# Two normalisations opened by a rough mean, a gather on chip, and hidden chunks in buffers of their own

## The chip, the core and the metric

The kernel runs on one core of one Trainium2 chip. The metric is the device time of one execution in microseconds (us), the median of several. Engines are named as in the profile: PE is TensorE (its weight loads are PEld), DVE is VectorE, ACT is ScalarE, POOL is GpSimd, and SP issues most DMAs.

## The reference

One inference step of a two-layer decoder on 264 token rows (256 of a prompt, 8 samples) of 1024 features, all in float32. What matters here is the end of each sub-layer and the start of the mixture of experts:

```python
def _layernorm(x, g, b):
    mu = jnp.mean(xf, -1, keepdims=True)
    var = jnp.mean(jnp.square(xf - mu), -1, keepdims=True)
    return (xf - mu) * lax.rsqrt(var + EPS) * g + b
...
x = _layernorm(ALPHA * x + mix, ln1_g, ln1_b)        # after each mixer
ffn = (silu(x @ w1) * (x @ w3)) @ w2                  # layer 0: dense, 2816 hidden
ffn = sum over the 2 of 8 experts that the router picks of the same form   # layer 1, 3584 hidden
x = _layernorm(ALPHA * x + ffn, ln2_g, ln2_b)
```

So there are four normalisations, numbered 0 to 3: after the first mixer, after the dense feed-forward, after the second mixer, and at the end.

## The kernel before

Everything is held with features on the 128 partitions: x is `X`, eight chunks of 128 features by 264 tokens. A float32 product is done as three passes on rounded halves (`split_product`, L555 to L557): weights and inputs are each split into a high part (rounded by ACT) and the rest (subtracted by DVE). ACT writes the high parts of a weight tile from the DMA ring into `whi` (`round_tile`, L1200), DVE the rests into `wlo` (`rest_of_tiles`, L1721); there are four such slots (`NSPLIT`), and a slot is free when PE has used tile g-4. SP fills a ring of four slots ahead. Each engine's order is written out by hand, and semaphores join them; a wait at the head of an engine holds all that stands behind it.

The stages are: input projection of layer 0 with its recurrences, output projection (`TOUT0`, eight tiles `mix 0..7`), normalisation 0, w1 and w3 of the dense layer (44 tiles), w2 (22 chunks f of the hidden layer, all eight outputs side by side in the eight PSUM banks), normalisation 1, input projection of layer 1 with its recurrences, output projection (`TOUT1`), normalisation 2, router, eight experts, normalisation 3.

A normalisation runs like this. For every tile that is done, DVE writes `R = ALPHA*X + mix` (`residual`, L1944). Then PE sums the eight chunks of `R` over the partitions by products with a matrix of ones (L802, ordinary float32, two passes a chunk), DVE subtracts the mean (L1961), ACT squares (L1375), PE sums the squares (L807), ACT makes the reciprocal root by Ln and Exp (L1383, L1386), DVE scales by it and the gain (L1972), ACT adds the shift and rounds to `Xh` (L1390), DVE writes the rest `Xl` (L1976), and PE starts the next projection.

In the dense layer the hidden chunks are rounded into `Xh` and `Xl`, the buffers that the w1 and w3 products read (`round_hidden`, L1410, and `rest_of_hidden`, L1997), so the first of them waits until the last product with w3 is done (`wait_h_free`).

After normalisation 2 PE makes the router's logits (L1027) and turns X to token rows (L1036). ACT copies these to `xtok` (L1214, from L1656 on) and sends them to `xrows` in HBM (L1657); for that it first waits until DVE has updated the eight sample states (L2167, `cnew_ready`), which POOL then stores (L2501, 4 MB, `o_Cs`). DVE ranks the tokens and builds a 0/1 matrix `G` of the first expert's tokens (L2345), PE multiplies it with the token numbers (`pick`, L1063), DVE makes row numbers of that, POOL fetches these rows from HBM by an indirect DMA (L2505), PE turns them back (`gather`, L1070), ACT and DVE split them (L1667, L2379), and the first expert starts (`begin`). The seven later gathers run under an expert's products.

Of the kernel before, what the change touches and what calls it, by code (L numbers as in the profile page):

```python
# [32 lines left out]
P = 128  # L33
D = 1024
# [45 lines left out]
TURN_BANK, SLOT_BANK = 6, 7  # L80
# [47 lines left out]
def decoder_step(nc, A):  # L128

    ctx = ExitStack()  # L130
    with ctx:
# [37 lines left out]
        nm = sb("nm", [P, N])  # L169
        lbt = sb("lbt", [P, 3, HG])  # L170
# [53 lines left out]
        vrows = nc.dram_tensor("vrows", (NS, D), F32).ap()  # L224
        yh0 = in_arena("yh0", [P, KD * N], F32R, YH_AT)
# [7 lines left out]
        def chunks(t):  # L233
# [105 lines left out]
                                                                  sem("rstd_ready"), sem("scaled"), sem("x_ready"))  # L339
        silu_ready, h_ready = sem("silu_ready"), sem("h_ready")  # L340
# [90 lines left out]

        def wait_slot_used(eng, load):

            eng.wait_ge(low_ready, last_tile[load] + 1)

        def wait_tile_used(eng, g):
# [4 lines left out]
            elif name[1] < FD - 1:  # L441
# [91 lines left out]
        def _(pe):  # L533
# [39 lines left out]
            def projection_by_inputs(first, last, stage):  # L573
# [4 lines left out]
                for c in range(KD):  # L578
                    pe.wait_ge(xl_ready, KD * stage + c + 1)
                    w = slice(c * P, (c + 1) * P)  # L580
                    for g in range(first, last):
                        mm = split_product(outs[g - first], whi[:, g % NSPLIT, w], wlo[:, g % NSPLIT, w], hi[:, c, :], lo[:, c, :],
                                           c == 0, c == KD - 1)
                        if c == KD - 1:
                            done(mm)
# [211 lines left out]
            def layernorm(n):  # L797

                out = job(("mean", n)) if n < 3 else bank[0]
                for k in range(KD):  # L800
                    pe.wait_ge(r_ready, KD * n + k + 1)
                    mm = pe.matmul(out[:, 0:N], ones, R[:, k, :], start=(k == 0), stop=(k == KD - 1))  # L802
                mm.then_inc(psum_ready, 1)
                out = job(("var", n)) if n < 3 else bank[1]
                for k in range(KD):
                    pe.wait_ge(sq_ready, KD * n + k + 1)
                    mm = pe.matmul(out[:, 0:N], ones, SQ[:, k, :], start=(k == 0), stop=(k == KD - 1))  # L807
                mm.then_inc(psum_ready, 1)

            projection(TOUT0, T13, 1)  # L810
            layernorm(0)


# [4 lines left out]
            for f in range(FD):  # L818
# [3 lines left out]
                for j in range(KD):  # L822
                    if f == 0:
                        outs.append(job(("mix", 1, j))[:, 0:N])
                    w = slice(j * P, (j + 1) * P)
                    mm = split_product(outs[j], whi[:, g % NSPLIT, w], wlo[:, g % NSPLIT, w], Xh[:, f % KD, :], Xl[:, f % KD, :],
                                       f == 0, f == FD - 1)
# [1811 lines left out]
```

## Time and profile before

| | us |
|---|---|
| runs | 1608.77, 1603.55, 1603.0 |
| median of the runs | 1603.55 |
| the profiled execution | 1608.27 |
| its span, first to last instruction | 1606.3 |
| PE busy | 1520.6 (95%) |
| DVE busy | 1274.2 (79%) |
| ACT busy | 1098.1 (68%) |
| DMA, mean over the span | 284 GB/s |

The profiled execution is one run with records of every instruction; its times are read as they are, and its total stands 4.7 us over the median of the runs. A busy share is a mean over stages that have different limits, so the stages are read one by one. PE's matmuls are pipelined, so its rows give the end of one with its latency; the pace is the distance of two starts.

### The profile page before, as it was taken

Reading aid. Unit: us, or ns where it says so; the run is one execution under the profiler, and the core shown is the slowest. Engines: PE = TensorE matmul, PEld = TensorE weight load, DVE = VectorE, ACT = ScalarE, POOL = GpSimd, SP = SyncE. Lnnn points to the kernel's source line nnn. Section 1 sums busy time; section 2 is a strip of 40 time slices with the busy share of each in tenths; the row PEclk is TensorE's granted clock in tenths of the full one; section 3 lists DMA queues with packets and bytes.
Section 4 is the critical chain, followed back from the end, with each engine's and each line's share of the span. In section 5 each row is a group of like instructions: output and inputs, shape, how many; then the busy total and the mean of one; then the engine's idle time right before and its main releaser. Section 6 shows DMA issues by size and latency. Waiting matters only on the chain.

```text
span 1606.3 us, 24275 instructions
## 1 busy us (share of the span) xinstructions
PE 1520.6 (95%) x8501; PEld 1316.3 (82%) x8501; DVE 1274.2 (79%) x1566; ACT 1098.1 (68%) x1387; POOL 32.9 (2%) x45
## 2 busy tenths in 40 slices
PE   6999899998889858999999999999999999999996
PEld 6888899998778846888888888888888888888885
DVE  4634566655755666999999999999999999999995
ACT  5436544444745745788788788788788888878884
POOL 0000000000001110000000000000000000000000
PEclk9999999999989988999999999999999999999998
DMA  8431655553424636999999999999999999999991
GB/s 331 151 128 67 184 184 184 210 216 138 176 104 158 221 149 233 374 381 350 370 379 346 377 379 347 376 370 348 379 379 354 367 376 352 373 378 354 371 371 57
DMA packets 54591, 455.52 MB, mean 284 GB/s; under 512 B 6992, under 2 KB 7192, under 8 KB 22272
## 3 DMA queue, kind: packets, MB, share of 16 engines
q1 hardware_dynamic: 47888, 423.74, 69.1%
q0 software_dynamic: 4096, 21.07, 3.7%
q10 hardware_dynamic: 2544, 9.86, 1.6%
q8 instruction: 41, 0.67, 0.2%
q14 instruction: 22, 0.18, 0.0%
HBM read 444.03 MB, written 10.62 MB: 283 GB/s over the span
## 4 chain that ended last, share of the span: by engine, by line
PE 80%; issue 12%; DVE 3%; ACT 2%; DMA 1%; ACTq 0%; POOL 0%; DVEq 0%; SPq 0%; POOLq 0%
PE bank L555 24%; PE bank L556 24%; PE bank L557 24%; PE bank L1100 1%; PE bank L802 1%; DMA arena<-xrows,row_at 1%; PE bank L550 1%; PE bank L671 1%; DVE wlo L1721 1%; DMA ring<-in_w_in 1%; ACT whi L1200 1%; PE bank L807 0%; PE bank L1070 0%; DVE arena L2024 0%; PE bank L1063 0%
## 5 line engine op out<-in xcount | busy, mean ns | idle before, releaser
L2297 DVE TENSOR_TENSOR wlo<-ring,whi 128x1024 fp32r<-128x1024 f32 x672 | 808.2, 1223 | 56.7 <-ACT whi L1644 14.5
L1644 ACT ACTIVATE whi<-ring 128x1024 fp32r<-128x1024 f32 x672 | 712.4, 1065 | 184.3 <-PE bank L557 182.4
L555 PE MATMUL bank<-whi,high 128*128 128x512 f32 x1344 | 531.7, 396 | 1.4 <-DVE low L2379 1.4
L557 PE MATMUL bank<-whi,low 128*128 128x512 f32 x1344 | 524.9, 391 | 0.0
L556 PE MATMUL bank<-wlo,high 128*128 128x512 f32 x1344 | 524.3, 390 | 0.0
L555 PE MATMUL bank<-high,whi 128*128 128x264 f32 x1008 | 298.3, 296 | 28.8 <-DVE wlo L1721 12.8
L557 PEld LDWEIGHTS bank<-whi,low 128*128 128x128 f32 x1344 | 252.8, 188 | 53.5
L555 PEld LDWEIGHTS bank<-whi,high 128*128 128x128 f32 x1344 | 253.1, 188 | 53.0 <-DVE low L2379 1.8
L556 PEld LDWEIGHTS bank<-wlo,high 128*128 128x128 f32 x1344 | 253.3, 188 | 50.7
L556 PE MATMUL bank<-low,whi 128*128 128x264 f32 x1008 | 292.9, 291 | 0.0
L557 PE MATMUL bank<-high,wlo 128*128 128x264 f32 x1008 | 292.6, 290 | 0.0
L1721 DVE TENSOR_TENSOR wlo<-ring,whi 128x1024 fp32r<-128x1024 f32 x134 | 161.9, 1224 | 143.3 <-ACT whi L1200 138.2
L1200 ACT ACTIVATE whi<-ring 128x1024 fp32r<-128x1024 f32 x134 | 141.6, 1060 | 162.1 <-PE bank L557 155.7
L555 PEld LDWEIGHTS bank<-high,whi 128*128 128x128 f32 x1008 | 197.6, 196 | 36.9 <-issue 23.2
L556 PEld LDWEIGHTS bank<-low,whi 128*128 128x128 f32 x1008 | 197.6, 196 | 0.1
L557 PEld LDWEIGHTS bank<-high,wlo 128*128 128x128 f32 x1008 | 196.4, 195 | 0.0
L1214 ACT ACTIVATE arena<-bank 128x264 f32<-128x264 f32 (+5 forms) x79 | 33.2, 435 | 45.9 <-PE bank L557 37.9
L1985 DVE TENSOR_TENSOR arena<-arena,bank 128x264 f32<-128x264 f32 x22 | 9.5, 430 | 45.9 <-PE bank L557 39.6
L2412 DVE SCALAR_TENSOR_TENSOR arena<-arena,bank 128x512 f32<-128x512 f32 x56 | 41.6, 743 | 0.0
L2417 DVE TENSOR_TENSOR low<-bank,high 128x512 fp32r<-128x512 f32 x56 | 38.3, 684 | 0.0
L1677 ACT ACTIVATE arena<-bank 128x512 f32<-128x512 f32 x56 | 32.7, 583 | 2.3 <-PE bank L557 2.3
L1100 PEld LDWEIGHTS bank<-con,arena 128*128 128x128 f32 x224 | 28.0, 141 | 7.0
(324 smaller groups left out, 969.2 us busy)
## 6 DMA issues: line engine op xcount, KB each, us to landing
ring<-in_w_moe SPq DMA_DIRECT2D x224, 1536.0 KB, 8.4
ring<-in_w_in SPq DMA_DIRECT2D x25, 1024.0 KB, 5.1
ring<-in_w SPq DMA_DIRECT2D x22, 1024.0 KB, 4.8
ring<-in_w SPq DMA_DIRECT2D x7, 1536.0 KB, 6.7
ring<-in_w_out SPq DMA_DIRECT2D x4, 1536.0 KB, 6.6
state<-in_state ACTq DMA_DIRECT2D x1, 4096.0 KB, 12.7
arena<-vrows POOLq DMA_DIRECT2D x8, 512.0 KB, 5.8
o_Cs<-state POOLq DMA_DIRECT2D x1, 4096.0 KB, 12.1
```

Of the source, the lines that this page charges most:

```text
L555: pe.matmul(out, xh, wh, start=start, stop=False)
L556: pe.matmul(out, xh, wl, start=False, stop=False)
L557: return pe.matmul(out, xl, wh, start=False, stop=stop)
L1100: mm = pe.transpose(bank[TURN_BANK][:, i * P:(i + 1) * P], hb[:, i * P:(i + 1) * P], ident)
L1200: A_(whi[:, g % NSPLIT, :], ring[:, load % RING, part * D:(part + 1) * D], ACT.Copy).then_inc(high_ready, 1)
L1214: return A_(out, see(act, name)[0:rows, 0:n], func, **kw)
L1644: A_(whi[:, g % NSPLIT, :], ring[:, s % RING, (g % 3) * D:(g % 3 + 1) * D], ACT.Copy).then_inc(whi_ready, 1)
L1677: A_(sE, bank[2 * (b % 2)], ACT.Silu).then_inc(silE_ready, 1)
L1721: V.tensor_tensor(wlo[:, g % NSPLIT, :], ring[:, load % RING, part * D:(part + 1) * D], whi[:, g % NSPLIT, :].bitcast(F32), ALU.subtract). ...
L2297: V.tensor_tensor(wlo[:, g % NSPLIT, :], ring[:, s % RING, (g % 3) * D:(g % 3 + 1) * D], whi[:, g % NSPLIT, :].bitcast(F32), ALU.subtract) ...
L2412: V.scalar_tensor_tensor(out=hb, in0=sE, scalar=slot[:, 1:2], in1=bank[2 * (b % 2) + 1], op0=ALU.mult, op1=ALU.mult).then_inc(hb_ready, 1)
L2417: V.tensor_tensor(hTl[:, b % 2].rearrange("p f n -> p (f n)"), bank[TURN_BANK], hTh[:, b % 2].bitcast(F32).rearrange("p f n -> p (f n)"), ...
```

## The change

1. **Normalisations 0, 1 and 2.** Once chunks 0 and 1 are done, PE multiplies them by `part` (all 1/256): their mean over 256 features, the `shift`. DVE takes `ALPHA*X - shift` for two chunks at once (`base`) and adds each `mix` when its tile is done (`centred_residual`), and takes the shift off chunks 0 and 1 afterwards (`centred_first`). ACT squares each chunk as it comes. The mean and the variance are corrected at the end: var = sum of squares/1024 less the square of the remaining mean. In 0 and 2 DVE adds up chunks and squares, and PE sums only what is left (`out_projection`); in 1 PE sums the chunks between and behind the last products. DVE subtracts the remaining mean in pairs and multiplies by the root, and ACT applies gain and shift and writes `Xh` and `X` by turns.
2. **Start of the next projection.** The first three tiles' products with the high input wait for `Xh` alone, those with the rest follow.
3. **End of the dense down projection.** The last two hidden chunks go output by output, so the outputs end one after another, not together.
4. **First three hidden chunks.** They are rounded into a buffer of their own (`first_h`), in the last three rounds of the w1 and w3 stage.
5. **First expert's gather.** PE multiplies `xtok` by `G` (24 float32 products of 128 columns) in place of the indirect DMA; `pick(0)` follows, into bank 5. The copies to `xrows` stay, since later experts' gathers use them.
6. **Sample states.** The updates of samples 5, 6 and 7 stand behind normalisation 2 on DVE, no longer within it.

```diff
...
+        first_h = in_arena("first_h", [P, 2 * HAHEAD * N], F32R, VB_AT)[:, :].rearrange("p (i f n) -> p i f n", i=2, f=HAHEAD)
+        def hidden_parts(f):
+            return (first_h[:, 0, f, :], first_h[:, 1, f, :]) if f < HAHEAD else (Xh[:, f % KD, :], Xl[:, f % KD, :])
...
@@ PE
+            def shift_sum(n):
+                pe.wait_ge(part_ready, 1)
+                wait_taken(pe, ("mix", n, 1))
+                for k in range(2):
+                    pe.wait_ge(r_ready, KD * n + k + 1)
+                    mm = pe.matmul(shift_bank(n)[:, 0:N], part[:], R[:, k, :], start=(k == 0), stop=(k == 1))
+                mm.then_inc(shift_ready, 1)
+            def open_square_sums(n):
+                pe.wait_ge(based, 3 * (n + 1))
+                pe.wait_ge(shifted, n + 1)
+                job(("var", n))
+            def out_projection(first, stage, n):
+                projection(first, first + 3, stage)
+                shift_sum(n)
+                projection(first + 3, first + KD - 1, stage)
...
+                open_sums(n)
+                open_square_sums(n)
+                pe.wait_ge(low_ready, g + 1)
...
+                    if i == 5:
+                        pe.wait_ge(dsum_ready, n // 2 + 1)
+                        pe.matmul(bank[J[("mean", n)] % 8][:, 0:N], ones, SQ[:, 7, :], start=True, stop=False)
+                done(mm)
+                pe.wait_ge(sqsum_ready, n + 1)
+                pe.matmul(bank[J[("var", n)] % 8][:, 0:N], ones, SQ[:, 0, :], start=True, stop=False)
+                done(centred_sum(n, 7))
+                done(square_sum_of(n, 7, stop=True))
...
+            def gather_first():
+                pe.wait_ge(g_ready, 1)
+                pe.wait_ge(xtok_ready, 6)
+                for k in range(KD):
+                    for t, (_, n) in enumerate(TT):
+                        mm = pe.matmul(bank[GATHER_BANK[k // 4]][:, (k % 4) * P:(k % 4 + 1) * P], xtok[0:n, t, k * P:(k + 1) * P],
+                                       G[0:n, t, :], start=(t == 0), stop=(t == 2))
...
@@ ACT
+            def deviation(n):
+                see(act, ("mean", n))
+                act.wait_ge(sqsum_ready, n + 1)
+                A_(SQ[:, 2, :], bank[J[("mean", n)] % 8][:, 0:N], ACT.Square, scale=1.0 / D).then_inc(meansq_ready, 1)
+                act.wait_ge(var_ready, n + 1)
+                own.settle(A_(nm[:], nm[:], ACT.Ln, bias=eps))
+                A_(nm[:], nm[:], ACT.Exp, scale=-0.5).then_inc(rstd_ready, 1)
...
@@ DVE
+            def sum_to_fifth(n):
+                dve.wait_ge(r_ready, KD * n + 6)
+                own.settle(V.tensor_tensor(SQ[:, 6:8, :], R[:, 2:4, :], R[:, 4:6, :], ALU.add))
+                own.settle(V.tensor_tensor(SQ[:, 7, :], SQ[:, 6, :], SQ[:, 7, :], ALU.add))
...
+            def layernorm(n, g=None):
+                see(dve, ("var", n))
+                dve.wait_ge(meansq_ready, n + 1)
+                V.scalar_tensor_tensor(out=nm[:], in0=bank[J[("var", n)] % 8][:, 0:N], scalar=1.0 / D, in1=SQ[:, 2, :],
+                                       op0=ALU.mult, op1=ALU.subtract).then_inc(var_ready, 1)
+                own.settle(V.tensor_scalar(SQ[:, 3, :], see(dve, ("mean", n))[:, 0:N], 1.0 / D, None, ALU.mult))
...
+                own.start(less_mean(n, 0))
...
+                own.start(less_mean(n, 2))
+                own.wait()
+                dve.wait_ge(rstd_ready, n + 1)
+                scale(n, 0)
...
+            def out_tile(n, k, g=None, state=None):
+                if k < 2:
+                    residual(n, k)
+                else:
+                    if k % 2 == 0:
+                        base(n, k)
+                    centred_residual(n, k)
+                    if k == 3:
+                        centred_first(n)
+                if g is not None:
+                    rest_of_tiles(g, g + 1)
+                if state is not None:
+                    new_sample_state(*state)
+                if k == 5:
+                    sum_to_fifth(n)
+                if k == 6:
+                    sum_to_sixth(n)
+                    first_squares(n)
+                    own.settle(more_squares(n))
+                    last_squares(n)
...
             layernorm(2)
+            for b in range(5, NS):
+                new_sample_state(b, 0, MH)
...
@@ POOL
-            pool.wait_ge(row_ready, 1)
-            fetch_rows()
...
```

PE at the end of the dense down projection, before (`whi` and `wlo` are the weight halves, `high` and `low` the hidden chunk's, `con` the ones; x8 is eight of a kind):

```order
L555 MATMUL bank<-high,whi 128x264
L556 MATMUL bank<-low,whi 128x264
L557 MATMUL bank<-high,wlo 128x264
L802 MATMUL bank<-R,con 128x264 x8
L807 MATMUL bank<-SQ,con 128x264 x8
L555 MATMUL bank<-high,whi 128x264
```

And now, from the last output's last chunk on:

```order
L577 MATMUL bank<-high,whi 128x264
L578 MATMUL bank<-low,whi 128x264
L579 MATMUL bank<-high,wlo 128x264
L834 MATMUL bank<-R,con 128x264 x4
L840 MATMUL bank<-SQ,con 128x264 x2
L928 MATMUL bank<-SQ,con 128x264 x2
L604 MATMUL bank<-high,whi 128x264
```

Of the sixteen sums behind the last product eight are left; two more of the chunks and two products with `part` have moved in among the outputs.

PE from normalisation 2 to the first expert, before:

```order
L802 MATMUL bank<-R,con 128x264 x8
L807 MATMUL bank<-SQ,con 128x264 x8
L1027 MATMUL bank<-X,wrout 8x264 x8
L1036 MATMUL bank<-con,X 128x128 x8
L1043 MATMUL bank<-con,SQ 128x8 x2
L1043 MATMUL bank<-con,SQ 8x8
L1036 MATMUL bank<-con,X 128x128 x8
L1036 MATMUL bank<-con,X 8x128 x8
L1051 MATMUL bank<-arena,con 128x8 x6
L550 MATMUL bank<-arena,con 128x8 x3
L1063 MATMUL bank<-arena 128x2 x3
L1070 MATMUL bank<-con,arena 128x128 x8
```

And now:

```order
L872 MATMUL bank<-SQ,con 128x264
L834 MATMUL bank<-R,con 128x264
L840 MATMUL bank<-SQ,con 128x264
L1123 MATMUL bank<-X,wrout 8x264 x8
L1132 MATMUL bank<-con,X 128x128 x8
L1139 MATMUL bank<-con,SQ 128x8 x2
L1139 MATMUL bank<-con,SQ 8x8
L1132 MATMUL bank<-con,X 128x128 x8
L1132 MATMUL bank<-con,X 8x128 x8
L1147 MATMUL bank<-arena,con 128x8 x6
L572 MATMUL bank<-arena,con 128x8 x3
L1168 MATMUL bank<-arena 128x128 x24
```

Three sums stand where sixteen stood, and the 24 products with `G` where `pick` and the eight turns stood; `pick` comes after them.

DVE around normalisation 2, before (L2167 and L2413 are the state updates, four a sample):

```order
L1944 SCALAR_TENSOR_TENSOR R<-X,bank 128x264
L1961 SCALAR_TENSOR_TENSOR R<-bank,R 128x528 x4
L2167 SCALAR_TENSOR_TENSOR state<-arena,state 128x256 x12
L1972 SCALAR_TENSOR_TENSOR R<-R,vec,nm 128x264 x8
L2302 MEMSET arena 128x24
```

And now:

```order
L2097 TENSOR_TENSOR R<-R,bank 128x264
L2153 SCALAR_TENSOR_TENSOR nm<-bank,SQ 128x264
L2155 TENSOR_SCALAR SQ<-bank 128x264
L2136 TENSOR_TENSOR R<-R,SQ 128x528 x2
L2141 TENSOR_TENSOR R<-R,nm 128x264 x2
L2141 TENSOR_TENSOR R<-R,nm 128x528
L2136 TENSOR_TENSOR R<-R,SQ 128x528
L2141 TENSOR_TENSOR R<-R,nm 128x528
L2136 TENSOR_TENSOR R<-R,SQ 128x528
L2141 TENSOR_TENSOR R<-R,nm 128x528
L2413 SCALAR_TENSOR_TENSOR state<-arena,state 128x256 x12
L2555 MEMSET arena 128x24
```

The twelve updates have moved from before the scaling to behind it.

## Rows read from the trace of the kernel before

**Rows 1.** The profile's page: the span, and the chain that ended last, by engine

```profile
span 1606.3 us, 24275 instructions
...
PE 80%; issue 12%; DVE 3%; ACT 2%; DMA 1%; ACTq 0%; POOL 0%; DVEq 0%; SPq 0%; POOLq 0%
```

**Rows 2.** Stretches: length, busy PE, PEld, DVE, ACT, POOL; granted clock, DMA share, GB/s

```profile
187.00:194.00 7.00, 6.30 (x29) 6.33 (x30) 5.83 (x14) 4.98 (x12) 0.00 (x0) 0.51 1.01 201
...
322.00:327.00 5.00, 4.07 (x21) 4.10 (x22) 2.35 (x5) 0.00 (x0) 0.00 (x0) 0.66 0.78 297
...
405.00:409.00 4.00, 3.60 (x17) 3.63 (x18) 4.00 (x11) 2.27 (x6) 0.00 (x0) 0.57 0.01 4
...
608.00:617.00 9.00, 7.44 (x21) 5.91 (x22) 2.61 (x3) 2.26 (x3) 0.00 (x0) 0.50 0.00 0
...
675.71:797.25 121.54, 121.54 (x565) 101.02 (x564) 115.09 (x120) 98.33 (x103) 1.06 (x1) 1.00 0.95 367
```

**Rows 3.** Timeline around normalisation 0, PE: start, length, instruction, idle time before it

```profile
175.88 3.72 PE L802 MATMUL bank<-R,con 128*128 128x264 f32 x16
...
187.70 0.56 PE L555 MATMUL bank<-high,whi 128*128 128x264 f32 x1 [2.96 <-DVE low L1976]
```

**Rows 4.** The same timeline, DVE

```profile
171.43 1.23 DVE L1721 TENSOR_TENSOR wlo<-ring,whi 128x1024 fp32r<-128x1024 f32 x1 [1.33 <-ACT whi L1200]
...
172.57 0.42 DVE L1944 SCALAR_TENSOR_TENSOR R<-X,bank 128x264 f32<-128x264 f32 x1
...
174.32 1.23 DVE L1721 TENSOR_TENSOR wlo<-ring,whi 128x1024 fp32r<-128x1024 f32 x1 [1.33 <-ACT whi L1200]
...
179.64 2.55 DVE L1961 SCALAR_TENSOR_TENSOR R<-bank,R 128x528 f32<-128x528 f32 x4 [0.85 <-PE bank L802]
```

**Rows 5.** The same timeline, ACT

```profile
185.38 0.42 ACT L1386 ACTIVATE nm<-nm 128x264 f32<-128x264 f32 x1
```

**Rows 6.** Timeline from w3 to w2, PE

```profile
322.93 0.36 PE L555 MATMUL bank<-high,whi 128*128 128x264 f32 x1 [4.49 <-issue]
```

**Rows 7.** Timeline around normalisation 1, PE

```profile
388.64 0.28 PE L557 MATMUL bank<-high,wlo 128*128 128x264 f32 x1
...
391.82 5.48 PE L802 MATMUL bank<-R,con 128*128 128x264 f32 x16 [2.90 <-DVEq L1947]
...
405.40 0.50 PE L555 MATMUL bank<-high,whi 128*128 128x264 f32 x1 [2.96 <-DVE low L1976]
```

**Rows 8.** The same timeline, DVE

```profile
391.82 3.88 DVE L1944 SCALAR_TENSOR_TENSOR R<-X,bank 128x264 f32<-128x264 f32 x7 [0.15 <-DVE R L1944]
```

**Rows 9.** Timeline from normalisation 2 to the first expert, PE

```profile
566.43 3.72 PE L802 MATMUL bank<-R,con 128*128 128x264 f32 x16
...
579.58 5.37 PE L1027 MATMUL bank<-X,wrout 128*8 128x264 f32 x16 [4.29 <-ACT X L1392]
...
593.95 1.50 PE L1063 MATMUL bank<-arena 128*128 128x2 f32 x6 [3.09 <-DVEq L2347]
...
608.14 1.94 PE L1070 MATMUL bank<-con,arena 128*128 128x128 f32 x8 [12.70 <-DMA arena<-xrows,row_at]
...
611.50 0.79 PE L555 MATMUL bank<-whi,high 128*128 128x512 f32 x1 [1.41 <-DVE low L2379]
```

**Rows 10.** The same timeline, DVE

```profile
576.44 1.67 DVE L2167 SCALAR_TENSOR_TENSOR state<-arena,state 128x256 f32<-128x256 f32 x4 [0.22 <-DVE state L2167]
```

**Rows 11.** The same timeline, ACT

```profile
585.73 1.09 ACT L1214 ACTIVATE arena<-bank 128x512 f32<-128x512 f32 x2 [0.36 <-PE bank L1036]
...
588.64 1.88 ACTq L1657 DMA_DIRECT2D xrows<-arena  x1
...
590.57 0.21 ACT L1660 ACTIVATE arena<-arena 128x3 f32<-128x3 f32 x1 [2.10 <-issue]
```

**Rows 12.** The same timeline, POOL

```profile
578.46 0.54 POOL L2501 DMA_DIRECT2D o_Cs<-state  x1 [32.88 <-DVEq L2171]
```

**Rows 13.** DMA issues: count, KB, us from issue to landing

```profile
o_Cs<-state POOLq DMA_DIRECT2D x1, 4096.0 KB, 12.1
```

More of the change, by code:

```diff
@@ L578, in projection_by_inputs @@
                 for c in range(KD):
+                    w = slice(c * P, (c + 1) * P)
+                    pe.wait_ge(xh_ready, KD * stage + c + 1)
+                    for g, out in zip(range(first, last), outs):
+                        pe.matmul(out, whi[:, g % NSPLIT, w], hi[:, c, :], start=(c == 0), stop=False)
+                        pe.matmul(out, wlo[:, g % NSPLIT, w], hi[:, c, :], start=False, stop=False)
                     pe.wait_ge(xl_ready, KD * stage + c + 1)
[L580 to L583, printed above, removed]
+                    for g, out in zip(range(first, last), outs):
+                        mm = pe.matmul(out, whi[:, g % NSPLIT, w], lo[:, c, :], start=False, stop=(c == KD - 1))
                         if c == KD - 1:
@@ L817, in _ @@
             outs = []
-            for f in range(FD):
+            for f in range(FD - 2):
                 g = T2 + f
@@ new lines, in gained @@
+            def gained(n, k):
+                act.wait_ge(scaled, scaled_at(n, k))
+                gain, shift = vec_(LN_OF[n][0], k), vec_(LN_OF[n][1], k)
+                if n < 2:
+                    A_(Xh[:, k, :], R[:, k, :], ACT.Identity, scale=gain, bias=shift).then_inc(xh_ready, 1)
+                A_(X[:, k, :], R[:, k, :], ACT.Identity, scale=gain, bias=shift).then_inc(x_ready, 1)
+            def layernorm(n, g=None):
+                deviation(n)
+                for k in range(KD):
+                    gained(n, k)
+                    if k == 5 and n < 2:
+                        round_tile(g)
@@ new lines, in _, with round_hidden @@
+            for i in range(3):
+                round_tile(TOUT0 + i + NSPLIT)
+            square(0, 2)
+            round_tile(TOUT0 + 3 + NSPLIT)
+            for k in (3, 0, 1):
+                square(0, k)
+            for i in range(4, KD - 1):
+                round_tile(TOUT0 + i + NSPLIT)
+                square(0, i)
+            nc.scalar.preload_act_table_set("natural_log_exp_and_others")
+            square(0, 7)
+            layernorm(0, T13 + 3)
+            def round_hidden(f):
+                act.wait_ge(h_ready, f + 1)
+                if f < HAHEAD:
+                    act.wait_ge(snew_ready, 3)
+                else:
+                    wait_h_free(act, f)
+                A_(hidden_parts(f)[0], hT[:, f, :], ACT.Copy).then_inc(hh_ready, 1)
@@ L1701, in _ @@
             expert(more * NE + (NE - 1), last=True)
-            layernorm(3)
+            for k in range(KD):
+                if k % 2 == 0:
+                    act.wait_ge(centred, k // 2 + 1)
+                A_(SQ[:, k, :], R[:, k, :], ACT.Square).then_inc(sq_ready, 1)
+            nc.scalar.preload_act_table_set("natural_log_exp_and_others")
+            act.wait_ge(psum_ready, NJOB + 2)
+            own.settle(A_(nm[:], bank[1][:, 0:N], ACT.Ln, scale=1.0 / D, bias=eps))
+            A_(nm[:], nm[:], ACT.Exp, scale=-0.5).then_inc(rstd_ready, 1)
+            for k in range(KD):
+                act.wait_ge(scaled, len(SCALE_PARTS) * 3 + k + 1)
+                A_(X[:, k, :], R[:, k, :], ACT.Identity, bias=vec_(LN_OF[3][1], k)).then_inc(x_ready, 1)
         @block.vector
```

339 lines of the change are left out of this document (217 added, 122 removed).

## The prediction

> **What bounds the kernel now.** I read the page's chain of waits first: 80% of the span ends on PE and 12% on issue [rows 1]. So the second step was to see whether PE has room inside its stages. The table of stretches says no for the longest: one expert's period is 121.54 us, PE is busy in all of it at clock 1.00, DVE in 115.09, the DMA engines at a share of 0.95 [rows 2]. Eight such periods make 972 us, and whatever starts them earlier is kept whole. Third, I read the timeline where PE stops: around normalisations 0, 1 and 2, from w3 to w2, and before the first expert [rows 3, 6, 7, 9]. There the reader sees not only a pause but a slow time behind it: 0.51, 0.66, 0.57 and 0.50 of full clock [rows 2], so 1.2 of 2.4 GHz for most of these stretches, always after PE has stood still. A stop costs its pause and then part of a slow stretch.
>
> **Bases.** Durations come from the profiled execution: span 1606.3 [rows 1] and about 2.0 around it, 1608.27. The median of the runs is 4.7 lower, 1603.55; the sum is taken from the profile and set against the median. About 8 us (0.5%) is what a measurement can tell from no change.
>
> **Normalisation 0.** Before: tile 7's products end at 175.9, sixteen instructions make eight chunk sums in 3.72, so 0.465 a chunk [rows 3], and w1 starts at 187.70: 11.8 us. Now:
> - The shift adds two chunk products, 0.93, on PE before tile 3.
> - PE stands at `open_square_sums` before tile 7, since `based` wants the third `base`. On DVE that stands behind tile 5's weight rest (start 171.43, 1.23 long) and `sum_to_fifth` (two operations, about 0.64 and 0.42, by the 528-wide at 2.55/4 = 0.64 and the 264-wide residual at 0.42 [rows 4], with completions 1.2), and lasts 0.64. PE finishes a tile in 2.89 (distance of the two weight rests [rows 4]). From tile 5's end the `base` ends after about 4.35, tile 6 after 2.9: a wait of 1.4. Behind it stand all of tile 7 and the sums, so it counts whole. Were `base` done in time it would be 0; one more weight rest ahead of it makes it 2.6.
> - The product with `dsum` between: 0.47. Together tile 7 ends 2.8 later.
> - Behind it: the last centred chunk and its square about 1.0, three sums 1.4, so the variance at +2.5; `nm` 0.45, Ln and Exp 0.42 each [rows 5], scaling 0.42 and ACT's Xh 0.5, with hand-overs (0.13 of completion seen between 0.42 and 0.55 [rows 4, 8], somewhat more between engines; an estimate) +5.95. DVE's `less_mean` (0.64 twice) lies beside Ln and Exp.
>
> Before 11.8, now 2.8 + 5.95 = 8.75: gain 3.0, with 0 to 5 as ends. Both restarts follow a pause of about 3 (2.96 before [rows 3]), so I give the slow stretch behind them no gain.
>
> **From w3 to w2.** The 4.49 idle [rows 6] is there because the first chunk must overwrite what w3 reads. With `first_h` three chunks are rounded in w3's last rounds, 3 x 24 products or three times a tile's 2.89 [rows 4], time enough for the fourth. The idle goes, and with no pause the stretch of 5.0 at 0.66 [rows 2] runs full: 0.34 x 5 = 1.7. Gain 6.1. Ends: 4.0 if the last of the three chunks comes late, 6.5.
>
> **Normalisation 1.** Before: the last product ends at 388.92, 405.40 is the restart, 16.5; in it 2.90 idle, seven residuals one behind the other at 0.55 [rows 8], and sums at 0.68 a chunk (5.48 for eight [rows 7]), since the clock was low after the pause. Now the last two hidden chunks go output by output, and DVE's and ACT's work on outputs 0 to 6 lies beside PE's products. PE adds the shift (0.93) and two centred sums (0.93) among them, so it ends at about 390.8; eight sums at 0.465 with no long pause ahead, and the last chunk's residual and square, lead to 395; the chain above without the sums (3.4) to 398.3. Gain 7.1. Ends: 5.3 with sums at 0.68, 9 if the shift hides.
>
> **Normalisation 2 and the router.** Same form as normalisation 0: tile 7 ended 566.43 and now 4.1 later (0.93, a wait of 2.1 since state updates of 0.42 each [rows 10] stand on DVE among the tiles too, 0.47, and 0.6 for `dsum`), variance at 573.1, scaling from 575.4 to 579.5. Logits begin some 3 us before 579.58 [rows 9]. But the twelve updates now stand behind scaling: 12 x 0.42 and completions 5.6, so they end at 585.1, where they ended at 578.11 [rows 10]. ACT's first copies to `xtok` wait for them; they began at 585.73, because of PE's turns [rows 11]. The earlier router is thus almost given back: 585.2 for 585.73, gain 0.5.
>
> **First gather.** Before: `pick` starts 593.95 and the first expert 611.50, with 12.70 of PE waiting for the rows from HBM [rows 9]. Now the indirect fetch is off this path (its next use is the second expert, 120 us later). 24 products of 128 columns: 0.465 x 128/264 = 0.225 each, 5.4 at full clock, 10.8 at half. PE has waited before it (3.09 [rows 9]), as ahead of the slow stretches of 3.4 to 6.8 us worth of work above; I take 5 of it slow, 7.9. With the split (1.45 by the 1.41 [rows 9]) and start at 593.45, the expert begins at 602.8: 8.7 earlier. Its first 5.4 us ran at 0.50 [rows 2]; now PE comes from products, so half of it, 2.7, comes back. Gain 11.4, the 0.5 included; ends 8.9 and 14. The expert's first weight halves are made by ACT and DVE beside these products; both had most of 608 to 617 free (2.26 and 2.61 busy of 9 [rows 2]), so I count them as hidden. Each microsecond that they come later than 602.8 would count.
>
> **Sum.** 3.0 + 6.1 + 7.1 + 11.4 = 27.6. From 1608.27: 1580.7; from the median: 1576.
>
> **Rivals.**
> - *A: ACT held at its second issue to `xrows`.* The issue at 588.64 lasted 1.88 and ended at 590.52 [rows 11]; the 4 MB store `o_Cs`, issued at 578.46 and landing after 12.1 [rows 12, 13], ended at 590.56. If ACT's issue waits for that store, the store is now issued 7.0 later, ACT's Exp of the router (590.57 [rows 11]) comes at 597.6 instead of 590.1, and 7.5 of the gain go: 1583.5. For: the two ends agree within 0.1, and ACT's idle before Exp is put to issue. Against: no semaphore joins them, and two issues in a row could fill 1.88 each by themselves. The Trainium skill, "DMA: Bandwidth & Descriptors", section "Queues, rings and completion order", has each DMA engine take turns between queues packet by packet, by which a store on another queue doesn't block this one; no row here shows such turns, and by that rule the time stays at 1576.
> - *B: DVE's chains are longer.* Normalisations with small DVE operations in series, each with its completion, lose half of 3.0 + 7.1: 1581. For: DVE is busy 5.83 of 7 in the restart of normalisation 0 [rows 2] and writes Xl there. Against: the durations come from rows.
> - *C: no slow clock in the gather*, 2.5 less, 1573.5; with a restart at full clock in normalisation 0 (7 us at 0.51, 3.4) 1570. For: PE makes its turns shortly before. Against: all four restarts above were slow.
> - *D, the other side: the weight stream becomes the bound.* The place is the experts: 367 GB/s x 121.54 is 44.6 MB each, at a share of 0.95 [rows 2]. It decides once a period passes 121.54 + 27.6/8 = 125.0, packets 8% slower; at 10% slower it is 0.95 x 1.10 x 121.54 = 127.0, 8 x 5.5 = 44 later, 1620. For: only 5% are spare. Against: the change leaves the stream alone, and PE showed no gap in that period. The Trainium skill, "DMA: Bandwidth & Descriptors", section "Where 436 GB/s comes from", lets the HBM side bind at about 358 GB/s, which would make 124.6 a period and 1600; the row's 367 is above it, and the measurement decides.
> - *E: it does not do what it says*, where the waits at `open_square_sums` and at the updates eat the normalisations (0 for 0 and 2, half for 1): 27.6 - 3.0 - 3.5 - 0.5, 1583; no row speaks for it but DVE's load.
>
> **How the numbers follow.** Forecast 0.46, A 0.25, B 0.11, C 0.10, E 0.04, D 0.04 (the page's rule in it 0.01). The time is the forecast's, 1576, its own range 1570 to 1581. The range reaches to C's 1570 with a little for both restarts, and past A to A with B, 1583.5 + 5: 1568 to 1590. What is left out is D and bigger misses on either side. Faster by over 0.5% (under 1595.5) are all cases but D and part of the misses: 0.93; within 0.5% 0.04; slower 0.03.
>
> **What would show it.** PE waits 1 to 2 us before tile 7 in normalisations 0 and 2, and restarts 8 to 9 us after the old place of tile 7's end; no idle between w3 and w2, and clock 1.00 there; about 9.4 from the old end of the last output to w's restart in normalisation 1. ACT's second issue to `xrows`: some 1.9 long if the forecast holds, ending with `o_Cs` if A does. 24 products in 5.4 (C), 7.9 or 10.8. An expert's period still 121.5; if it is longer, D or contention is at work. Wrong is the prediction where the restart of an expert waits for weights, or where ACT's copies come after 590.

## The result: a third of the forecast gain, and where the rest went

| | before | changed |
|---|---|---|
| median of the runs, us | 1604.1 (4 runs, 1603.0 to 1608.77) | 1594.03 (4 runs, 1591.72 to 1594.92) |
| ratio, 95% interval | | 0.9926 [0.9908, 0.9944] |
| span of the profiled execution | 1606.3 | 1592.9 |

The kernel is 10 us faster; the forecast was 1576, 28 us faster, with a range from 1568. On the page of the changed kernel, the span and the chain that ended last:

```profile
span 1592.9 us, 24340 instructions
...
PE 80%; issue 13%; DVE 5%; ACT 1%; DMA 1%; POOL 0%; DVEq 0%; SPq 0%; ACTq 0%; POOLq 0%
```

The chain reads as before [rows 1], 80% on PE, with a little more on issue and DVE. What moved is seen by following one instruction of PE from stage to stage:

| PE starts | before | changed | earlier by |
|---|---|---|---|
| w1 | 187.70 | 185.37 | 2.3 |
| w2 | 322.93 | 315.87 | 7.1 |
| input projection of layer 1 | 405.40 | 391.73 | 13.7 |
| router's logits | 579.58 | 564.79 | 14.8 |
| first product with G | 593.95 | 581.96 | 12.0 |
| first expert | 611.50 | 598.40 | 13.1 |
| end of the span | 1606.3 | 1592.9 | 13.4 |

So all of the gain stands by the start of layer 1. From the logits to the first expert the changed kernel takes 33.6 us where the kernel before took 31.9: the place from which 11 of the 28 us were to come is 1.7 us longer. The profile's 13.4 is more than the medians' 10; run 12 below shows that two executions of one kernel can differ by as much.

The stages in the table of stretches (length, then busy PE, PEld, DVE, ACT, POOL; granted clock, DMA share, GB/s):

```profile
185.40:192.00 6.60, 6.60 (x34) 6.60 (x35) 5.30 (x12) 6.60 (x13) 0.00 (x0) 0.59 0.99 227
...
318.00:323.00 5.00, 5.00 (x43) 5.00 (x43) 4.97 (x7) 2.43 (x4) 0.00 (x0) 1.00 0.76 259
...
391.73:395.73 4.00, 4.00 (x20) 3.96 (x21) 3.71 (x9) 4.00 (x9) 0.00 (x0) 0.57 0.02 4
...
582.00:597.00 15.00, 15.00 (x49) 11.41 (x49) 6.15 (x13) 2.05 (x3) 0.00 (x0) 0.50 0.64 239
...
598.40:603.40 5.00, 5.00 (x13) 3.94 (x13) 2.27 (x4) 1.06 (x1) 0.00 (x0) 0.50 0.00 0
...
604.00:609.00 5.00, 5.00 (x23) 4.13 (x22) 3.63 (x4) 4.30 (x4) 0.00 (x0) 1.00 0.34 96
...
662.30:783.80 121.50, 121.50 (x563) 100.98 (x563) 115.05 (x120) 98.34 (x103) 1.05 (x1) 1.00 0.95 367
```

The last line is one expert, 121.50 us as before [rows 2], so an earlier start is kept. From w3 to w2 (second line) the clock is 1.00 where it was 0.66. But all 15 us of the gather and the 5 us behind it ran at 0.50.

The timeline of PE in the changed kernel (start, length, instruction, idle time before it) at normalisation 0, at the start of w2, and at normalisation 1:

```profile
175.86 0.36 PE L577 MATMUL bank<-yh,whi 128*128 128x264 f32 x1 [1.55 <-issue]
...
180.18 0.71 PE L872 MATMUL bank<-SQ,con 128*128 128x264 f32 x2 [0.73 <-DVE SQ L2121]
...
185.37 0.56 PE L604 MATMUL bank<-high,whi 128*128 128x264 f32 x1 [3.58 <-ACT high L1495]
...
315.87 0.28 PE L577 MATMUL bank<-first_h,whi 128*128 128x264 f32 x1
...
383.34 0.29 PE L579 MATMUL bank<-high,wlo 128*128 128x264 f32 x1
...
384.79 1.36 PE L834 MATMUL bank<-R,con 128*128 128x264 f32 x4 [0.27 <-DVE R L2097]
...
391.73 0.36 PE L604 MATMUL bank<-high,whi 128*128 128x264 f32 x1 [3.54 <-ACT high L1495]
```

The 1.55 is the wait at `open_square_sums`, the 3.58 and 3.54 are the chains from the last sum to the first `Xh`, which take the place of 2.96 and of the sums before it [rows 3, 7]. At 315.87 there is no idle time where 4.49 stood [rows 6].

The same timeline of PE from normalisation 2 to the first expert (L1123 the logits, L1147 the ranks, L1168 the gather, L1159 `pick`, L577 the expert):

```profile
557.30 0.71 PE L869 MATMUL bank<-SQ,con 128*128 128x264 f32 x2 [0.74 <-DVE SQ L2132]
...
564.79 2.01 PE L1123 MATMUL bank<-X,wrout 128*8 128x264 f32 x8 [3.59 <-ACT X L1496]
...
576.19 2.42 PE L1147 MATMUL bank<-arena,con 128*128 128x8 f32 x12 [3.53 <-DVEq L2578]
...
581.96 15.03 PE L1168 MATMUL bank<-arena 128*128 128x128 f32 x48 [2.06 <-DVEq L2600]
...
596.91 1.53 PE L1159 MATMUL bank<-arena 128*128 128x2 f32 x6
...
598.40 0.79 PE L577 MATMUL bank<-whi,high 128*128 128x512 f32 x1
```

DVE there, the first four and the last four of the twelve late updates:

```profile
567.61 1.67 DVE L2413 SCALAR_TENSOR_TENSOR state<-arena,state 128x256 f32<-128x256 f32 x4
...
571.38 1.67 DVE L2413 SCALAR_TENSOR_TENSOR state<-arena,state 128x256 f32<-128x256 f32 x4 [0.21 <-DVE state L2413]
```

ACT there, a copy to `xtok`, the second issue to `xrows`, and the router's Exp:

```profile
573.31 1.08 ACT L1319 ACTIVATE arena<-bank 128x512 f32<-128x512 f32 x2 [3.40 <-DVEq L2417]
...
576.21 0.34 ACTq L1792 DMA_DIRECT2D xrows<-arena  x1
...
576.60 0.21 ACT L1795 ACTIVATE arena<-arena 128x3 f32<-128x3 f32 x1 [0.56 <-ACT arena L1319]
```

On PE the wait of 12.70 for rows from HBM [rows 9] is gone, and 48 passes, 0.313 us each on average, stand in its place, with a wait of 3.53 for the selection that was 0.56 before. On DVE the updates run from 567.61 to 573.05; only then can ACT copy tokens (573.31, after 3.40 of waiting) and DVE select. ACT's second issue to `xrows` took 0.34, not 1.88 [rows 11]. The ranks on PE in the kernel before:

```profile
588.68 1.50 PE L1051 MATMUL bank<-arena,con 128*128 128x8 f32 x12 [0.56 <-DVEq L2325]
```

### The profile page after: what moved, and what is told of

The parts are those of the page before. It is cut to its first block, busy times and chain, and to the rows that moved or that the text cites. A ratio compares the mean times of both kernels' runs of the same rounds, so it can differ in the third digit from the quotient of the medians.

```text
span 1592.9 us, 24340 instructions
## 1 busy us (share of the span) xinstructions
PE 1521.7 (96%) x8493; PEld 1315.3 (83%) x8493; DVE 1291.0 (81%) x1591; ACT 1102.5 (69%) x1390; POOL 26.7 (2%) x45
## 4 chain that ended last, share of the span: by engine, by line
PE 80%; issue 13%; DVE 5%; ACT 1%; DMA 1%; POOL 0%; DVEq 0%; SPq 0%; ACTq 0%; POOLq 0%
PE bank L577 23%; PE bank L578 23%; PE bank L579 23%; PE bank L1207 1%; PE bank L1168 1%; PE bank L572 1%; DVE state L2413 1%; PE bank L696 1%; DVE wlo L1866 1%; DMA ring<-in_w_in 1%; PE bank L604 0%; ACT whi L1305 0%; PE bank L605 0%; PE bank L608 0%; DVE arena L2270 0%
## 5 line engine op out<-in xcount | busy, mean ns | idle before, releaser
L577 PE MATMUL bank<-whi,high 128*128 128x512 f32 x1344 | 531.7, 396 | 0.0
L577 PE MATMUL bank<-high,whi 128*128 128x264 f32 x936 | 276.0, 295 | 20.8 <-DVE wlo L1866 12.7
L577 PEld LDWEIGHTS bank<-whi,high 128*128 128x128 f32 x1344 | 253.0, 188 | 51.2 <-issue 0.3
L578 PE MATMUL bank<-low,whi 128*128 128x264 f32 x936 | 270.0, 288 | 0.0
L579 PE MATMUL bank<-high,wlo 128*128 128x264 f32 x936 | 269.6, 288 | 0.0
L577 PEld LDWEIGHTS bank<-high,whi 128*128 128x128 f32 x936 | 181.2, 194 | 28.6 <-issue 14.9
L578 PEld LDWEIGHTS bank<-low,whi 128*128 128x128 f32 x936 | 181.4, 194 | 0.2
L579 PEld LDWEIGHTS bank<-high,wlo 128*128 128x128 f32 x936 | 180.3, 193 | 0.0
## 6 DMA issues: line engine op xcount, KB each, us to landing
o_Cs<-state POOLq DMA_DIRECT2D x1, 4096.0 KB, 12.2
```

The costliest lines, as they stand in the source:

```text
L577: pe.matmul(out, xh, wh, start=start, stop=False)
L578: pe.matmul(out, xh, wl, start=False, stop=False)
L579: return pe.matmul(out, xl, wh, start=False, stop=stop)
```

## The experiments

All are the changed kernel with one edit, but for the last. Ratios are to the kernel before, run on the same chip in the same session; medians of before there were 1604 to 1608. "Router" is the distance from the first logit product to the first expert's first product on PE, which takes out what happened earlier in an execution.

| run | edit | median, us | ratio, 95% interval | router, us |
|---|---|---|---|---|
| | before | 1604.1 | 1 | 31.9 |
| | changed | 1594.0 | 0.9926 [0.9908, 0.9944] | 33.6 |
| 1 | first rows from HBM again | 1594.8 | 0.9941 [0.9921, 0.9962] | 33.4 |
| 2 | added products in the router | 1585.0 | 0.9887 [0.9862, 0.9912] | 27.6 |
| 3 | three updates on POOL | 1601.4 | 0.9974 [0.9965, 0.9984] | 29.8 |
| 4 | added products at norms 0 and 1 | 1591.1 | 0.9914 [0.9898, 0.9931] | 33.8 |
| 5 | added products inside the gather | 1603.0 (one run) | | 40.3 |
| 6 | 2 and 4 | 1585.5 | 0.9873 [0.9840, 0.9907] | 27.7 |
| 7 | three updates left out | 1586.7 (one run) | | 29.1 |
| 8 | 6, and two places in layer 1 | 1584.2 | 0.9860 [0.9830, 0.9890] | 27.7 |
| 9 | updates moved behind G | 1589.7 | 0.9896 [0.9876, 0.9917] | 29.1 |
| 10 | 8 and 9 | 1580.9 | 0.9845 [0.9826, 0.9864] | 26.4 |
| 11 | part 4 undone | 1598.4 | 0.9953 [0.9935, 0.9971] | 33.9 |
| 12 | the kernel before, again | 1605.1 (one run) | | 31.2 |

**Run 1: is the gather on chip worth anything?**

```diff
-            gather_first()
-            pick(0, FIRST_SLOT_BANK)
+            pick(0)
+            gather(0)
@@ POOL
+            pool.wait_ge(row_ready, 1)
+            fetch_rows()
```

> The changed kernel with its part 5 undone: the first expert's rows come from HBM by the indirect DMA again, all else stays. Theory T (the gather on chip took 15.0 us, since PE stood at half clock for all 48 passes of 0.313 each, so it replaced 17.55 us from pick to expert by 16.44): 1.1 slower than the changed kernel, about 1595. Rival S (the gather saved what was forecast, 10.9 us, and the loss lies in another part): about 1605, as slow as the kernel before.

Ratio and router distance are those of the changed kernel (33.4 and 33.6). PE's timeline there:

```profile
579.06 1.50 PE L1159 MATMUL bank<-arena 128*128 128x2 f32 x6 [1.96 <-DVEq L2602]
...
592.51 1.94 PE L1177 MATMUL bank<-con,arena 128*128 128x128 f32 x8 [11.95 <-DMA arena<-xrows,row_at]
...
595.86 0.80 PE L577 MATMUL bank<-whi,high 128*128 128x512 f32 x1 [1.41 <-DVE low L2634]
```

From `pick` to the expert it is 16.8 us with a wait of 11.95 on a DMA, and 16.4 with products. Rival S falls: the gather did not save what was forecast.

**Run 2: what sets the gather's price?** `warm(out, n)` multiplies a stable chunk by the ones n times, 264 columns each, into a bank that the next product overwrites.

```diff
             out = job("rank")
+            warm(out, 7)
             pe.wait_ge(sel_ready, 1)
...
+                wait_bank(J["lg"] % 8)
+                warm(bank[J["lg"] % 8], 4)
                 pe.wait_ge(g_ready, 1)
```

> The changed kernel with eleven idle-time products of 264 columns added on PE: seven in its wait for the selection (3.53 us), four in its wait for G (2.06 us). Theory T (half clock after these waits sets the gather's price): granted clock 1.00 in the gather, a pass 0.157 in place of 0.313, 7.5 us in place of 15.0, and the first expert starts at full clock (2.6 more): about 1584. Rival K (weight loads or the traffic on the chip set the pass, whatever the clock): gather still about 15, 1594 to 1596.

PE's timeline in run 2 (L614 are the added products, L1175 the gather):

```profile
576.15 3.01 PE L614 MATMUL bank<-SQ,con 128*128 128x264 f32 x8 [0.74 <-DVEq L2599]
...
578.96 9.08 PE L1175 MATMUL bank<-arena 128*128 128x128 f32 x48
...
589.46 0.50 PE L577 MATMUL bank<-whi,high 128*128 128x512 f32 x1 [0.57 <-DVE low L2639]
```

Its stretches, with the columns as above:

```profile
577.00:580.00 3.00, 3.00 (x11) 2.26 (x9) 2.42 (x12) 3.00 (x4) 0.00 (x0) 0.50 0.92 393
...
581.00:587.00 6.00, 6.00 (x36) 4.55 (x34) 3.11 (x4) 0.60 (x1) 0.00 (x0) 1.00 0.86 291
...
591.00:594.00 3.00, 3.00 (x8) 2.33 (x8) 1.23 (x1) 1.09 (x2) 0.00 (x0) 0.50 0.00 0
...
595.00:600.00 5.00, 5.00 (x23) 4.13 (x23) 4.11 (x5) 4.22 (x5) 0.00 (x0) 1.00 0.51 174
```

The same 48 passes took 9.08 us in place of 15.03. In the 6 us at clock 1.00 one chunk of the gather, six passes, took 1.05 us, where it takes 1.87 at half clock. Theory T holds for the clock: the price follows it, though not by half (0.176 a pass, not 0.157).

The kernel is 9 us faster than the changed one by the medians, 6 by the ratios, and its router is 6.0 shorter. The other 3 us are not the edit's: the spans of the two profiles differ by 9.8, and 3.0 of that lie ahead of w1 (182.41 for 185.37), where the two kernels are alike. There, at 57.8 to 61.1 and at 88.5 to 91.8, the granted clock was 0.50 in the changed kernel and 1.00 in run 2. The second fall stands behind 3.3 us of products of 64 and 128 columns, without a pause.

Two details of theory T do not hold. The clock had fallen by 577.0, although the seven products had filled the long wait: it fell behind the 18 short passes of 8 columns, with 0.42 of idle time ahead of them and 0.74 behind, and rose at 580.4, 4.3 us after the four other products began. And it fell again at 590.7, 1.2 us after the expert's first product, until 594.1, so of the 2.6 us at the expert about 1 came back.

**Runs 3, 7 and 9: what do the late state updates cost?**

```diff
@@ run 3: samples 5, 6, 7 on POOL, as two operations each
+                Pv.tensor_tensor(vk, vk, bc(ki[:, :, b:b + 1], [P, MH, MDV]), ALU.mult).then_inc(cnew_pool, 1)
+                Pv.tensor_tensor(Cs[:, :, b, :], vk, Cs[:, :, b, :], ALU.add).then_inc(cnew_pool, 1)
@@ run 7
-                new_sample_state(b, 0, MH)
@@ run 9
+SAMPLE_ORDER = [0, 1, 2, 3, 7, 4, 5, 6]
-            act.wait_ge(cnew_ready, NS)
+            act.wait_ge(cnew_ready, 5)
...
+            new_sample_state(5, 0, MH)
             split_gathered(0, 0, 1)
+            new_sample_state(6, 0, MH)
             split_gathered(0, 1, 2)
...
+            new_sample_state(7, 0, MH)
```

> The changed kernel with the state updates of samples 5, 6 and 7 on POOL, which stood idle for 41 us there, in place of DVE behind normalisation 2. If these updates on DVE (5.4 us) delay the selection and so G: G some 3 us earlier, about 1591. Rival: POOL is slow or slows DVE, and ACT's copies and the selection wait for it instead: 1594 or more.

> The changed kernel without the state updates of samples 5, 6 and 7 (left out, nothing in their place). If these updates, 5.4 us of DVE between the scaling and the selection, hold G up: PE's wait for the selection (3.53) goes and ACT's copies of the tokens start at once, and G comes 3 to 4 us nearer to the start of the logits (17.2 us in the changed kernel). Rival (PE's turns and ACT's copies set G anyway): 17 us as before.

> The changed kernel with the updates of three samples moved once more: sample 7 takes the place of sample 4 within the second output projection, and samples 4, 5 and 6, whose rows nothing overwrites until the first expert runs, stand behind the first expert's weight halves on DVE. If the updates ahead of the selection cost 4.5 us, as leaving them out showed: 1589.5, the gather still 15 us at half clock. Rival (the moved updates hold up the split of the gathered rows, and the first expert with it): 1593 to 1596.

Run 3 is slower than the changed kernel. The router is 3.8 us shorter, but DVE, working beside POOL, fell behind within the output projection, and PE waited 13.07 us there. POOL's timeline in run 3, the two operations of one sample:

```profile
549.94 2.02 POOL L2769 TENSOR_TENSOR arena<-arena 128x1024 f32<-128x1024 f32 x1 [16.51 <-ACTq L1645]
...
552.04 2.41 POOL L2771 TENSOR_TENSOR state<-arena,state 128x1024 f32<-128x1024 f32 x1
```

DVE's timeline beside it, four updates and a sum:

```profile
549.32 5.42 DVE L2414 SCALAR_TENSOR_TENSOR state<-arena,state 128x256 f32<-128x256 f32 x4 [0.21 <-DVE R L2098]
...
561.95 2.62 DVE L2127 TENSOR_TENSOR SQ<-R 128x528 f32<-128x528 f32 x1
```

Four updates that take 1.67 alone took 5.42: two took 0.48 each, the other two lasted until the POOL operation beside them had ended. One sum of 528 columns took 2.62 where the changed kernel has 0.71, while an addition with one input from PSUM, under a POOL operation too, kept its 0.43. The Trainium skill, "SBUF — State Buffer", section "SBUF: two separate sides", has DVE operations with two inputs in SBUF and POOL operations that read SBUF lock one shared pair of ports against each other; these rows agree with it.

Without the updates (run 7) PE waits 0.56 for the selection, and G comes 12.7 us after the first logit product, not 17.2. PE's timeline, ranks and gather:

```profile
570.58 1.50 PE L1147 MATMUL bank<-arena,con 128*128 128x8 f32 x12 [0.56 <-DVEq L2580]
...
574.82 15.03 PE L1168 MATMUL bank<-arena 128*128 128x128 f32 x48 [2.06 <-DVEq L2602]
```

So they cost 4.5 us. Run 9 takes the same 4.5 off the router with nothing left out, and its ratio says 4 to 5 us. In both the gather took 15.03, as long as in the changed kernel, although between the logits and the gather PE waited only 0.56 and 2.06.

**Run 5: do the gather's own products bring the clock back?**

```diff
                     if k % 4 == 3:
                         mm.then_inc(xg_psum, 1)
+                    warm(bank[J["lg"] % 8], 1)
```

> The changed kernel with one product of 264 columns behind each of the eight chunks of the gather and none ahead of it. Theory T2 (the gather's short products, with their weight loads in between, do not bring the clock back, products of 264 columns do): the clock comes back inside the gather, some 5 us after its start, and the gather with its eight added products takes about 14. Rival L (the clock stays low because PE stood still before, whatever it multiplies now): 8 x (6 x 0.313 + 0.93) = 22.5 us, all at 0.50.

The stretches of run 5, the gather, the expert's first 5 us, and a later one:

```profile
582.70:604.80 22.10, 22.10 (x64) 16.93 (x65) 6.44 (x15) 3.06 (x4) 0.00 (x0) 0.50 0.42 162
...
606.20:611.20 5.00, 5.00 (x13) 3.98 (x13) 2.30 (x4) 1.06 (x1) 0.00 (x0) 0.50 0.00 0
...
613.00:616.00 3.00, 3.00 (x15) 2.46 (x14) 2.34 (x3) 2.25 (x3) 0.00 (x0) 1.00 0.36 82
```

The clock stayed at 0.50 for 22.1 us, the number of rival L and not mine: one product of 264 columns behind every six passes of the gather did not bring it back. L's reason fails all the same. The clock rose some 6 us after the expert's products began (606.20 to 612.2), as it did in the changed kernel after 5.5 (598.40 to 603.9) and in runs 7 and 9 after 3, and in run 2 it rose 4.3 us after the four added products began. It does depend on what PE multiplies. What in the gather's passes denies it was not taken apart: their few columns, the weight load in each, the stops where the rows of the weights change (shown further down), or the values of `G`, almost all 0.

**Runs 4, 6, 8, 10: filling other waits.**

```diff
@@ run 4, projection_by_inputs
                 outs = [job(tiles[g][2])[:, 0:N] for g in range(first, last)]
+                warm(outs[0], 7)
@@ run 8
+                    if g == TOUT1:
+                        warm(out, 11, X)
...
                 out = job("fw")
+                warm(out, 8, X)
```

> The changed kernel with seven products of 264 columns in PE's waits of 3.58 and 3.54 us ahead of the restarts of normalisations 0 and 1. If the slow stretches behind them (0.59 of full clock over 6.6 us; 3.8 us at half) come from PE standing still: both restarts at 1.00, 2.7 + 1.9 = 4.6 less, about 1589. Rival: the clock falls there whatever PE does, or the added products are late themselves: 1594 to 1596.

> The changed kernel with the added products at both places: in the waits of the router, and ahead of the restarts of normalisations 0 and 1. If both act by the clock alone, they add: 9.0 and 3.0 less than the changed kernel, 1582. If one eats the other: 1585.

> As the kernel with both, and eleven such products in PE's wait of 5.21 us ahead of the second output projection and eight in its wait of 4.06 us in the second layer's recurrence. If a slow stretch stands behind every wait because PE stood still: 2.1 + 3.5 less, about 1576. Rival (the recurrence there is bound by DVE and ACT, so a faster PE waits elsewhere): 2 less at most, 1580.

> The kernel with added products at all four places, with the updates moved as in the run before, and with one added product (not seven) in the wait for the selection, which then lasts some 0.6 us. If both gains add: 4 less than 1584.2, about 1580. Rival (with only five added products the clock does not come back before the gather, which then takes 15 us at half clock): 1586 to 1588.

Stretches of run 4, the 6.6 and 4.0 us behind both restarts:

```profile
184.77:191.37 6.60, 6.60 (x52) 6.40 (x53) 5.30 (x12) 6.60 (x13) 0.00 (x0) 1.00 1.01 231
...
389.42:393.42 4.00, 4.00 (x31) 3.80 (x32) 3.71 (x9) 4.00 (x9) 0.00 (x0) 1.00 0.02 4
```

1.00 where the changed kernel had 0.59 and 0.57. From w1's start to w2's, and from layer 1's first product to the logits, it is 1.7 us shorter each, 3.4 in all; where the other 1.2 of the expected 4.6 went was not traced. Run 6 has both effects in its trace (1.7 behind each restart, 5.9 in the router), but its four runs spread over 5 us and its interval holds run 2's ratio: by time it is inconclusive.

Run 8 gained 1.3 by the medians and nothing in its trace: from layer 1's first product to the logits it takes 171.4 us, as run 6 does. In the recurrence the wait that its products filled shrank from 4.06 (0.30 in run 10), and the next one, for DVE, grew from 4.21 to 5.79 (7.33 in run 10): the rival was right, DVE sets the pace there. The output projection began at full clock, but further on, at 548.1 to 554.8, the clock was 0.50, from a wait of 2.89 ahead of the last tile on. Behind the same wait it was 1.00 in run 6.

Run 10 is the fastest kernel, 1580.9: 13 us less than the changed kernel, 23 to 25 less than before. Its router is 1.3 us shorter than run 8's, not 4: the logits ran at half clock (0.50 at 557.4 to 564.1), and the four products ahead of the gather took 3.3 us where the wait in run 9 was 2.06. Its gather ran at full clock throughout:

```profile
574.77 8.40 PE L1180 MATMUL bank<-arena 128*128 128x128 f32 x48
...
575.00:583.00 8.00, 8.00 (x48) 6.18 (x46) 7.61 (x13) 1.38 (x2) 0.00 (x0) 1.00 0.53 187
```

**Run 11: part 4 undone.**

```diff
-            return (first_h[:, 0, f, :], first_h[:, 1, f, :]) if f < HAHEAD else (Xh[:, f % KD, :], Xl[:, f % KD, :])
+            return Xh[:, f % KD, :], Xl[:, f % KD, :]
```

> The changed kernel with part 4 undone: the first three hidden chunks share the buffers that w1 and w3 read, as before. By the forecast's term the wait of 4.49 and 1.7 us of half clock come back between w3 and w2: 6.1 to 6.4 slower, about 1600. Rival (the gain was taken back by DVE's and ACT's extra work in w3's last rounds): 1594 to 1596.

PE's timeline at the start of w2:

```profile
319.97 0.50 PE L577 MATMUL bank<-high,whi 128*128 128x264 f32 x1 [4.48 <-issue]
```

The idle 4.48 is back, and from w1's start to layer 1's first product it is 6.2 us longer (212.5 to 206.4). The medians say 4.4, with runs from 1595 to 1604.

**Run 12: the kernel before, again.**

> The kernel before, unchanged, for a second profiled execution. If the 3.3 us by which the two profiled executions differ more than the medians come from stages that the change leaves alone: a stretch ahead of 150 us is some 3 us shorter or longer than in the first profile, and from the end of w3 to the first expert the distances are the same within 0.5 us.

Up to 150 us the two profiles agree within 0.2, so I looked in the wrong place. The span is 3.2 us shorter, and 2.3 of it lie in layer 1's recurrence, in 451.95 to 457.66 (5.71 us) where the first profile, and that of the changed kernel, have 7.97 and 7.88. The granted clock there was 1.00 in run 12, 0.69 in the first profile and 0.70 in the changed kernel's. The first profile, then run 12:

```profile
451.70:459.67 7.97, 7.31 (x39) 5.43 (x39) 0.35 (x1) 1.94 (x3) 0.00 (x0) 0.69 0.27 112
...
451.95:457.66 5.71, 5.05 (x38) 4.00 (x39) 0.34 (x1) 1.93 (x3) 0.00 (x0) 1.00 0.39 160
```

Two profiled executions of one kernel differ by more than some of the terms of my sum, which is why the distances above are taken within one execution.

## Why the prediction was wrong

The step that failed is the price of the first gather: "24 products of 128 columns: 0.465 x 128/264 = 0.225 each, 5.4 at full clock, 10.8 at half", "I take 5 of it slow, 7.9", and behind it "now PE comes from products, so half of it, 2.7, comes back". Three things were wrong in it.

1. *The changes between weights of 128 rows and of 8 were left out.* A product is two passes, and each pass loads its own weights. A chunk has four passes with 128 tokens as the rows of the weights and then two with the last 8. Between passes of like rows the scaling by columns was right: they start 0.213 apart at half clock and 0.111 at full (run 10), where it gives 0.225 and 0.113. Six of them would make 1.28 and 0.67 us a chunk. But a chunk takes 1.87 and 1.05, and the difference lies around its two changes, from 128 rows to 8 and back. There the weight loads stop for 0.22, which they do not between like passes:

```profile
581.93 0.93 PEld L1168 LDWEIGHTS bank<-arena 128*128 128x128 f32 x4 [2.13 <-issue]
583.08 0.50 PEld L1168 LDWEIGHTS bank<-arena 8*128 8x128 f32 x2 [0.23 <-issue]
583.80 0.93 PEld L1168 LDWEIGHTS bank<-arena 128*128 128x128 f32 x4 [0.22 <-issue]
```

So the changes make 4.7 of the 15.0 us, and 3.0 of the 8.4 in run 10; what is left, 10.3 and 5.4, is near the forecast's 10.8 and 5.4. Why a change costs this is not shown: no run filled the last tile up to 128 rows. The Trainium skill, "TensorE: Matmul & The Clock Gate", section "LDWEIGHTS (loading the stationary operand)", says that a load's time goes by its columns and not by its rows; the 8-row loads here, 0.28 to 0.33 us like those of 128 rows, agree with it.
2. *It ran at half clock to its end.* I gave 5 us, by the slow stretches behind other restarts [rows 2]. Those were followed by dense products of 264 or 512 columns. The gather's passes did not bring the clock back, not even with a dense product after every six (run 5).
3. *The expert's slow start stayed*: 598.40 to 603.40 at 0.50, as before [rows 2]. Even where the gather ran at full clock, the clock fell behind it (run 2). The forecast counted on a fall only after PE has stood still; it also came behind short products.

Together: 11.4 forecast with the 0.5 of the router, so 10.9; measured 17.55 to 16.44 us, 1.1, and 0.3 behind it. That is 9.5 of the 14.2 us by which the profile's gain fell short: 7.1 for the gather itself (15.0 for 7.9), 2.4 at the expert.

The other terms, by the traces of the two kernels:

- *Normalisation 0*: 3.0 forecast, 2.3 measured; the wait before tile 7 was 1.55 for 1.4.
- *From w3 to w2*: 6.1 forecast; 4.7 of idle time and about 1.7 of half clock measured, 6.2 in run 11. Right.
- *Normalisation 1*: 7.1 forecast, 4.9 measured. PE's own part grew by 3.4 to the last output, not by 1.9: besides the 1.9 of added products it waited 1.0 for the residuals ahead of the shift, which I had not counted (the last 0.5 was not traced); the chain behind took 8.1 for 7.5, 0.27 of it a wait ahead of the last sums. The mechanism was right, the size not.
- *Normalisation 2 and the router*: 0.5 forecast, a loss of 1.4 measured: the second output projection starts 13.4 earlier, the first product with G 12.0. I had the updates as a delay for ACT's copies alone. They also stand ahead of the selection on DVE, and runs 7 and 9 put them at 4.5.
- *Rival A* (ACT held by the 4 MB store) did not come: the second issue took 0.34 with that store under way (from 573.40 for 12.2), and Exp came at 576.60 without delay. But the agreement of the two ends was no chance, for run 12 has it again, at 588.1 (the store issued at 576.01 lands after 12.1 there, too). What held the issue in the kernel before, and no longer does, stays open. ACT's second issue in run 12:

```profile
585.91 2.17 ACTq L1657 DMA_DIRECT2D xrows<-arena  x1
```

- *D* did not come either: 121.50 a period. *C* was the wrong way round, the clock was worse than forecast. *B*, which took half of the 10.1 of normalisations 0 and 1, came in part: 7.2 were measured. *E* came nearest, though not in its place: PE's waits at `open_square_sums` were about as forecast (1.55 and 2.88 for 1.4 and 2.1), the one behind the updates was not.

## What to carry to other kernels

Before small products take the place of a wait, look in the trace at the granted clock ahead of them and at the distance of two passes wherever the weights change their rows, not only between like ones: short passes can run at half clock from first to last. A wait that can't be removed can be filled with products of many columns that nobody reads, and what then follows can run at full clock (6 us here in the router, 3 at two restarts). They have to end before the wait would, no other engine may set the pace, and the clock can still fall at a later wait, as in run 8. Compare such edits by distances within one execution: the clock in stages that they leave alone moved the whole by 3 us. And work moved "behind" a step has to be followed on its own engine to the next thing that this engine owes to others.

## What the runs showed of the hardware that was not expected

- Float32 passes of 128 columns, each with its own weights, start 0.213 us apart at 1.2 GHz and 0.111 at 2.4 as long as the number of rows in the weights stays the same. Six of them with a change from 128 rows to 8 and back take 1.87 and 1.05, not 1.28 and 0.67 (the changed kernel, run 10). 15.0 us of them, PE counted as busy throughout, left the granted clock at 0.50.
- The clock also fell behind 18 passes of 8 columns with 0.42 and 0.74 us of idle time around them (run 2), and waits of 0.56 and 2.06 with such passes between were enough (run 7). It fell without any pause behind 3.3 us of products of 64 and 128 columns (88.5 in the changed kernel), and at the same place in run 2 it did not.
- A POOL operation of 128x1024 (2.0 to 2.4 us) beside DVE stretched four updates from 1.67 to 5.42 us (run 3), but not an addition that reads PSUM.
